# Issuing two 2 MB weight loads inside a loop over cache pages instead of behind it, in a one-core decoder step

## The reference

```
z = einsum('bsd,de->bse', rms_norm(x), w_in)        # q, k, v of 8 + 8 heads, forget logits
o_sb = stick_breaking(q_sb, k_sb_all, v_sb_all)     # 8 heads
o_fx = forgetting(q_fx, k_fx_all, v_fx_all, c)      # 8 heads, softmax with decay
y = concat(rms_norm(o_sb), rms_norm(o_fx)) @ w_out  # w_out is 2048 x 2048
h = x + y
f = hier_moe(rms_norm(h))                           # 32 experts, two of them per row
out = rms_norm(h + f)
```

## Time and profile before

| what | value |
|---|---|
| median of 3 runs | 1517.79 us (1516.69 to 1523.81) |
| span of the profiled execution | 1514.3 us |
| PE, DVE, ACT, POOL busy | 87%, 44%, 15%, 5% |
| DMA, mean over the span | 377 GB/s |
| read from HBM | 558.26 MB |
| page loop ends on PE | about 947 us |
| first expert matmul | 994.97 us |

### The profile page before, as it was taken

The page is one execution under the profiler, slowest core; times in us unless marked ns, Lnnn a source line. Parts: engine busy times, 40 slices in busy tenths (PEclk is TensorE's granted clock), DMA queues, the critical chain, the costliest instruction groups (busy, mean ns, idle before and its releaser), DMA issues. The chain is left out here.

```text
span 1514.3 us, 26133 instructions
## 1 busy us (share of the span) xinstructions
PE 1315.7 (87%) x8622; PEld 870.3 (57%) x8622; DVE 673.4 (44%) x4778; ACT 233.6 (15%) x453; POOL 75.4 (5%) x119
## 2 busy tenths in 40 slices
PE   7999788889789899856899987789999999999992
PEld 4678455566556566533667743466666565655561
DVE  4437855676676675677846466021000100000004
ACT  2111002112212212213011021101111010111011
POOL 1000000000000000001000001001100010001000
PEclk8899989899999999976999998979999999999997
DMA  9776999999999999999999989999999999999984
GB/s 302 248 260 229 385 397 391 396 383 381 382 377 390 383 379 392 387 405 398 351 403 402 401 320 390 399 414 379 422 428 428 427 424 423 422 419 414 416 341 178
DMA packets 170382, 570.39 MB, mean 377 GB/s; under 512 B 17401, under 2 KB 75562, under 8 KB 156954
## 3 DMA queue, kind: packets, MB, share of 16 engines
q1 hardware_dynamic: 145616, 541.70, 91.4%
q10 hardware_dynamic: 21762, 22.58, 4.3%
q0 software_dynamic: 2896, 4.86, 0.9%
HBM read 558.26 MB, written 15.67 MB: 379 GB/s over the span
## 5 line engine op out<-in xcount | busy, mean ns | idle before, releaser
L128 DVE CUSTOM_DVE_ANT_0 ws<-ws,xgT 128x128 f32<-128x128 f32 x1792 | 387.8, 284 | 204.7 <-DMA ws<-in_cache_fox_k 186.0
L979 PE MATMUL bank<-xn,ws 128*128 128x264 f32 x1152 | 289.9, 407 | 10.5 <-DMA ws<-in_w_in 10.5
L979 PEld LDWEIGHTS bank<-xn,ws 128*128 128x128 f32 x1152 | 223.0, 199 | 110.9 <-issue 54.8
L1912 PE MATMUL bank<-ws,xgT 128*64 128x256 f32 x1024 | 231.4, 386 | 16.7 <-DMA ws<-in_w_expert_up 12.1
L1914 PE MATMUL bank<-ws,xgT 128*64 128x256 f32 x1024 | 231.5, 386 | 0.0
L964 PE MATMUL bank<-ws,PR 128*32 128x512 f32 x1024 | 150.8, 668 | 78.3 <-DMA ws<-in_cache_fox_v 73.8
L1912 PEld LDWEIGHTS bank<-ws,xgT 128*64 128x64 f32 x1024 | 140.3, 139 | 104.6 <-issue 22.2
L128 DVE DVE_READ_ACCUMULATOR2_ANT Z<- 128x1 f32 x1792 | 141.8, 79 | 0.0
L1914 PEld LDWEIGHTS bank<-ws,xgT 128*64 128x64 f32 x1024 | 140.3, 139 | 0.0
L2113 DVE COPY gu<-bank 128x256 f32<-128x256 f32 x32 | 13.6, 425 | 269.4 <-PE bank L1914 269.4
L1084 PE MATMUL bank<-qo,ws 128*128 128x256 f32 x512 | 117.0, 387 | 6.2 <-DVE qo L1521 5.2
(11 more groups left out here) (433 smaller groups left out, 971.4 us busy)
## 6 DMA issues: line engine op xcount, KB each, us to landing
ws<-in_cache_sb_k SPq DMA_DIRECT2D x128, 512.0 KB, 9.1
ws<-in_cache_fox_k SPq DMA_DIRECT2D x128, 512.0 KB, 13.0
ws<-in_cache_sb_v SPq DMA_DIRECT2D x128, 512.0 KB, 9.2
ws<-in_cache_fox_v SPq DMA_DIRECT2D x128, 512.0 KB, 12.8
ws<-in_w_expert_gate SPq DMA_DIRECT2D x32, 2048.0 KB, 16.1
ws<-in_w_expert_up SPq DMA_DIRECT2D x32, 2048.0 KB, 20.0
ws<-in_w_expert_down SPq DMA_DIRECT2D x32, 2048.0 KB, 16.9
ws<-in_w_in SPq DMA_DIRECT2D x24, 2048.0 KB, 21.3
```

The costliest lines, as they stand in the source:

```text
L128: ins = dve.tensor_tensor_reduce(k, k, qb[:, (g * H + h) * HD:(g * H + h + 1) * HD], 1.0, 0.0, ALU.mult, ALU.add, Z[:, n % 2, g, h, t:t + 1])
L979: mm = pe.matmul(out[:, 0:T], w[:, c, m * P:(m + 1) * P], xn[:, c, :], start=(c == 0), stop=(c == KC - 1))
L1912: pe.matmul(bank[2 * k][0:SLOTS, 0:256], lhs, ws[:, wg, c * 256:(c + 1) * 256], start=(c == 0), stop=(c == KC - 1))
```

## The change

A step of SP's loop may now also issue a chunk: in step 109 it waits for `kused` 126 and issues chunk 0 into slot 0 (whose last pages are 124 and 125); in step 110 it waits for `kused` 128 and issues chunk 1 into slot 1. Both stand behind the value page of that step. The wait and the two loads behind the loop are gone. Nothing else is touched; no byte is loaded more or less.

```diff
 OWN = STEPS - 13
+REREAD = (STEPS - LEAD + 1, STEPS - LEAD + 2)
...
                 if s + LEAD < STEPS:
                     load_key_page(sp, S, kring, key_caches, ptr, s + LEAD, n_phys)
+                if s in REREAD:
+                    j = REREAD.index(s)
+                    sp.wait_ge(S["kused"], STEPS - 2 + 2 * j)
+                    load_out(sp, a, ws, W, j, j)
...
-            sp.wait_ge(S["kused"], STEPS)
-            for j in range(2):
-                load_out(sp, a, ws, W, j, j)
             sp.wait_ge(S["vused"], STEPS)
             for j in range(2, 4):
                 load_out(sp, a, ws, W, j, j)
```

## The result

The changed kernel is slower: 1529.06 us at the median (7 runs, 1524.42 to 1533.23) against 1517.79 us (7 runs, 1513.03 to 1523.81). The ratio is 1.0073 with an interval of 1.005 to 1.0096, so 11 us more, 8 to 15.

> The changed kernel once more, beside the next three: 9 to 13 us slower than before by every theory.

The account below looks back on a forecast made before the run. The prediction took the DMA engines as the bound, with PE also full in the experts. Page 127's delay of 7.7 us less 3.1 won behind the loop gave +4.6 on 1517.8, so 1522.4 us, range 1515.5 to 1529.

Parts of the forecast that it names:

- the bound: In page loop and experts the DMA engines are nearly full, so what shifts the first expert shifts the end.
- the old hole: Between 884 and 900 us, 6.5 us in which an average DMA engine has nothing to do; the edit's target.
- the delay at page 111: Behind the two moved chunks, value page 111 lands at 909.8 instead of 899.9, 9.9 us late.
- the 0.9 us for which the last engine is idle: Ahead of page 111, the hole's width on the slowest DMA engine, subtracted once from the chunks' full length.
- The rival by which every engine fills the hole: At 884 to 900 us, chunks use all 6.5 us: delay 4.3, change +1.2, time 1519.0 us; chance 0.20.
- d: Lateness of the last value page, 127: between 5.5 and 9.9 us, taken as 7.7.
- with pages queued up deeper these may close, all or none: From page 111 to page 127, short gaps of 4.4 us in all might vanish, reducing the 9.9 us delay.
- what is won behind the loop: Behind page 127, chunk 5 gains 3.1 us on the pages' delay, though the queue runs dry twice.
- rival 2: PE at half clock in four router steps behind page 111: 4.9 us more, change +9.5, time 1527.3 us; chance 0.18.
- its sign: Behind page 111, a PE clock near 0.5 for over 10 us would show the half-clock rival.
- the gap from 4.6 to 11 us: For the whole kernel, the forecast change was +4.6 us, from +2.4 to +6.8; 11 is the measured loss.
- All that leads from page 127 to sample_out is compute: Behind the page loop, this stretch shifts by the last page's delay, chunk 4's issue moving from 960.9 by 7.7 us.

Follow-up runs that it names:

- the next three: Three experiments run on the same chip as the changed kernel's second measurement, which gave 1527.9 us, ratio 1.008.
- the chunks twice: Changed kernel with chunks 0 and 1 loaded once more behind the loop, 4 MB more in all; ratio 1.0082 to the kernel before.
- PE kept busy: Changed kernel with matmuls of no use in PE's waits from page 110, in two extents; ratios 1.0039 and, to the end of sample_out, 1.0048 to before.
- the second trace: Profile of the changed kernel measured again, nothing altered: traced execution 1522.61 us; its runs have a median of 1527.9 us, ratio 1.008 to before.
- One chunk alone: Kernel before with only chunk 0 moved into step 109, or only chunk 1 into step 110; ratios 1.0034 and 1.0044.
- eight pages in stock: Kernel before with some value pages put in the key ring, up to eight under way, chunks 0 and 1 left behind page 127; ratio 0.9997.
- few matmuls to keep PE busy: Changed kernel with 5 unused matmuls ahead of page 110, 12 ahead of page 111, 6 ahead of the counts; ratio 1.0039 to before.
- the kernel before with PE kept busy: Kernel before with unused matmuls in PE's waits from step 118 to the end of sample_out, nothing else changed; ratio 0.9974.
- the first trace: Profile of the changed kernel's first measurement: traced execution 1532.39 us; its runs have a median of 1529.06 us, ratio 1.0073 to before.
- chunk 1 alone: Kernel before with only chunk 1 moved, issued in step 110, and chunk 0 left behind the loop; ratio 1.0044.
- the first try: Changed kernel with 10 unused matmuls ahead of page 110, 26 ahead of page 111, 14 ahead of the counts; ratio 1.0094 to before.

## Why the prediction was right or wrong

**Right: the bound, and where the edit acts.** The DMAs stayed full from 884 to 908, through the old hole, chunk 0 went out at 880.22 and chunk 1 at 890.46, SP's waits on `kused` held up nothing, and the new long issue on SP (3.93 us for half of page 111) left the DMAs busy: their share was 0.98 to 1.03 from 892 to 908.

**Right: the delay at page 111.** The forecast was 9.9 us, by taking each chunk's full length and giving back the 0.9 us for which the last engine is idle. Measured: 10.0 us in the changed kernel, 9.9 with the chunks twice, 10.0 and 9.9 with PE kept busy, 11.5 in the second trace. One chunk alone gave 6.1 and 4.5 where 4.5 was expected. The rival by which every engine fills the hole, and its 4.3 us, was wrong, in spite of a mean share of 0.12. Windows of 1 us of the kernel before, columns as in the earlier trace rows, show what that share was:

```profile
891.00:892.00 1.00, 1.00 (x6) 0.90 (x5) 0.93 (x8) 0.47 (x2) 0.00 (x0) 1.00 0.24 98
892.00:893.00 1.00, 1.00 (x6) 0.62 (x4) 0.24 (x2) 0.98 (x2) 0.00 (x0) 1.00 0.06 25
893.00:894.00 1.00, 1.00 (x9) 0.16 (x8) 0.79 (x3) 0.99 (x4) 0.00 (x0) 1.00 0.08 33
```

One engine of 16 is a share of 0.06, and a sixteenth of the 410 GB/s of a full stretch is 26 GB/s. So from 892 to 893, while pages 109 and 110 were still under way (they landed at 893.1 and 896.5), one engine's worth of work was all that went on. Which engine it is, and why it was behind, the trace doesn't tell.

**Wrong: d, the delay of page 127.** The step that failed is "with pages queued up deeper these may close, all or none", from which d was put between 5.5 and 9.9 us, and 7.7 was taken. It was 12.6 and 12.9 us, and 10.3 with the chunks twice, whose order on SP is the same up to page 127. The 4.4 us that the stretch had over the pure load time weren't short gaps that could close: from 900 to 944 the kernel before has a DMA share of 1.01, at 390 GB/s. And with eight pages in stock the stretch still takes 42.1 us, by the pace of the compute, so of the 45.1 us no more than 3 could be caught up, and d could hardly be under 7 us. Instead the stretch got longer, to 47.7, 46.5 and (chunks twice) 45.5 us; with PE kept busy it took 43.7 and 42.3. The new hole from 908 to 920 stands where the ring of four pages filled up behind PE. Half clock is only a part of that: page 112 needs weights that ACT makes after page 111 (the row at 913.49), and with few matmuls to keep PE busy, at a clock of 1.00, the shares of these stretches are still 0.83, 0.75 and 0.89. With PE kept busy d is 8.5 and 7.1 against before, and 8.3 against the kernel before with PE kept busy, near the 7.7.

**Mostly right: what is won behind the loop.** The forecast was 3.1 us; from sample_out to chunk 5 the traces have 1.7 and 2.6. Between the two kernels with PE kept busy, page 127 is 8.3 us late and chunk 5 is 4.7, so 3.6 are won. The two dry stretches of the queue are there, at 956 to 960 and 972 to 976.

**The time of rival 2 (0.18) came, its mechanism only in part.** It put PE at half clock in the four router steps and priced that at 4.9 us, for 1527.3. Both medians, 1529.06 and 1527.9, lie by this rival's time and not by the forecast's. But its slow router step (1.93 and 1.98 us) came in two steps of four in the first trace and in part of one in the second, and its sign, a clock near 0.5 for over 10 us behind page 111, stayed out: it was some 9 us in the first trace and some 3 in the second. From page 111 to page 116, so over the four router steps and one more, it takes 16.4 and 14.1 us, 14.5 before, and 13.3 with PE kept busy: 2 us over before in the first trace, nothing in the second. The rest of the half clock lies elsewhere, in pages 119 and 120 (the stretch from 936 to 940) and, in the first trace, in first_tokens. So that the rival's time fits is in part luck. The range reaches up to 1529 only because this rival was taken into it. The arguments that I held against the rival (matmuls bring the clock back, the ring takes up the delay) were too weak for 0.18. Whether the clock is the cause of all of the gap from 4.6 to 11 us stays open: keeping PE busy gave 4 to 6 us back in the changed kernel, but 3.9 us in the kernel before as well.

**Not thought of:** that the steps behind page 127 have two lengths. "All that leads from page 127 to sample_out is compute" let them shift as a block. In the first trace first_tokens took 9.88 us at half clock, in the second 7.39, so sample_out started 17.1 or 13.5 us behind page 127 (13.8 before); and the experts took 522.4 or 519.5 us from their first matmul to the end (519.3 before). The work is the same in both; from 960 to 964 the granted clock was 0.50 in the first and 1.00 in the second. The lateness of page 127 doesn't decide this by itself: with eight value pages, where that page is early, first_tokens takes 9.82 us too.

## What to carry to other kernels

A hole in the mean DMA share isn't free room: look at how late the transfers land that were issued before it. If one still lands at the hole's end, some engine has no hole (here the mean share fell to 0.06, one engine of 16), and whatever is queued ahead of the next urgent load delays it by its full length. Before you fill a hole, ask whether the stretch behind it is paced by loads or by compute; here page 127 could be had 2.3 us earlier, and the kernel was no faster for it. And a load that stands behind the last urgent one covers its use; moved ahead, it takes that cover away.

## What the runs showed of the hardware

- Half-clock stretches of PE (0.50) followed idle stretches of PE: one of 6.23 us ahead of page 111, but also two of 1.94 and 1.49 us, ahead of pages 124 and 125 with chunk 1 alone. The times of the same code differ: first_tokens took from 7.39 us at full clock to 10.23, the experts 518.3 to 519.5 or 521.7 to 522.4 us. Matmuls of no use in PE's waits made the kernel before faster by 0.26% (0.15 to 0.37).
- A matmul of 128x256 in float32 with a 128x128 weight is two records of 0.22 us in this trace: 12 of them took 5.45 us. This is what spoiled the first try.
- An issue on SP took longer when many loads were under way: 0.33 us for half a page in most rows, 3.93 us behind the two chunks. The DMAs stayed busy meanwhile.
- At the end of a long stretch of loads one DMA engine was behind the others: in the kernel before, the share at 892 to 893 was 0.06 of 16 engines, at 25 GB/s.
